# A two-block transformer kernel: x loaded in four parts between the weights and split from PSUM, the bias lines as one matmul, and the side work of the first projection in smaller steps

## The chip, the cores and the metric

One core of a Trainium2 chip runs the whole program. The metric is device time in microseconds (us) of that core, inputs in HBM to output in HBM; the kernel before has a median of 2737.01 us over 3 runs. Everything is float32 in and out. The matrix products run on TensorE (PE) as three products of split operands: a float32 number is written as hi + lo, and hi·hi, hi·lo and lo·hi are added up in PSUM. ScalarE (ACT) makes every hi, VectorE (DVE) every lo, SyncE (SP) issues the weight transfers.

## The reference, cut to what matters

The first block begins with a norm and one projection whose columns are q, k, v, u and g; the change touches this part and the small preparations for what follows it.

```python
a = rms_norm(h, attn_norm_g[i])                 # x is 256 x 2048
z = a @ w_in[i]
zq, zk, zv, zu, zg = jnp.split(z, splits, axis=-1)
...
bias = rel_bias[t5_bucket(kpos[None, :] - qpos[:, None])]   # 4 heads, depends on kpos - qpos only
logits = jnp.where(mask, logits + bias[None, :, None], NEG_INF)
...
o_gmlp = gmlp_spatial_gate(jax.nn.gelu(zu), jax.nn.gelu(zg), gmlp_ln_g[i], gmlp_ln_b[i], gmlp_ws[i], gmlp_b[i])
...
h = jnp.concatenate([meta, x], axis=1)          # second block: 16 meta tokens ahead
hn = rms_norm_2(h, norm_mix_g)
```

## The kernel before, in words

The program is a list of segments (`schedule`): `v`, `qk`, `g`, `u`, `out`, `f1_up0` and so on. A segment reads one activation buffer (`A` or `B`, hi and lo side by side) and works through its weights in pieces of 256 rows by 512 columns. One transfer from SP (`run` inside the `sync` block) brings two pieces (1 MiB) into one of 4 slots of `raw`. For each piece ACT copies `raw` to `hi` (`split` on ACT), DVE computes `lo = raw - hi` (`split` on DVE), both into rings of 4, and PE multiplies it (`piece`). In the `v` segment, the first, a piece is 12 matmuls of 512 columns, and a piece may start only when its `lo` is there. In `qk`, the second, a piece starts with its `hi`.

Every engine executes its own instructions strictly in the order written. `walk` writes that order for ACT and DVE: split up to three pieces ahead (`AHEAD`), at a group's end the evacuation, and after certain pieces the side steps that the table `SIDE` names, by segment and piece number. `run` on PE places the same side steps after the same pieces. So a side step on which PE waits holds up all matmuls behind it, and a step on which ACT waits holds up the hi of all later pieces. The `split` of piece n waits until piece n-4 has been used.

Before the first piece, x is transposed on PE to `h` (features on partitions), 32 transposes of 128x128: DVE copies PSUM to `h`, ACT makes the hi of `A` from `h` (`high_parts`), DVE the lo (`low_parts`). The gains are loaded ahead of x as nine small vectors, since `high_parts` scales by one of them.

The side steps of `v` before are these. `token_squares` and `token_rstd` make 1/rms of each token. `lines` builds for each head a line of 512 bias values, by four matmuls whose stationary operand repeats the head's 32 values 128 times; the result, the same line on all 128 partitions, goes to `line` and from there to the DRAM tensor `skew`, whose rows are 513 long. `read_bias` waits on ACT for that transfer (`skew_written`) and then reads `skew` back with a row step of 512, which shifts each row by one: this is `bias`. `row_rstd` turns 1/rms into a row, `turn_ws` transposes the gate weights and the meta tokens, `meta_rstd` makes 1/rms of the meta tokens, `lambda` the scalar of the attention.

Of the kernel before, what the change touches and what calls it, by code (L numbers as in the profile page):

```python
# [19 lines left out]
ALU = mybir.AluOpType  # L20
# [5 lines left out]
P = 128  # L26
D = 2048
# [25 lines left out]
V1N, V2N = 82, 96  # L53

# [54 lines left out]
def ffn(add, name, n, gate, up, down, kinds, layout):  # L109
# [37 lines left out]
    ("f1_up0", 6): ["ffn_rstd"], ("f1_up0", 7): ["settle"],  # L147
# [51 lines left out]
def bass_two_blocks(nc, ins, out):  # L199
    SEGS, TOTAL = schedule()  # L200

    with ExitStack() as ctx:
# [6 lines left out]
        def overlay(**shapes):  # L209
# [13 lines left out]
        line, _, = overlay(line=[P, HEADS, LINE], pad_line=[P, 1])  # L223
# [24 lines left out]
        _, relb_in, meta_in, vin1, vin2, relb, onehot, lamv, rb = overlay(  # L248
            v_skip=[P, 2048 - 8], relb_in=[32, HEADS], meta_in=[META, D], vin1=[V1N, P], vin2=[V2N, P], relb=[32, HEADS, P],
# [21 lines left out]
        consts_set, vecs_landed, early_landed = sem("consts_set"), sem("vecs_landed"), sem("early_landed")  # L271
        gmlp_normed = sem("gmlp_normed")
        left_scaled, right_scaled = sem("left_scaled"), sem("right_scaled")
        x_landed = [sem(f"x_landed{i}") for i in range(2)]
        skew_written, bias_landed, late_landed, stored = (
            sem("skew_written"), sem("bias_landed"), sem("late_landed"), sem("stored"))
        NVECS, NEARLY = 9, 9
# [28 lines left out]
        def _(sp):  # L306

            for name, src in (("attn", ins["attn_norm_g"][0]), ("ffn", ins["ffn_norm_g"][0]), ("fin", ins["final_norm_g"]),
                              ("mix2", ins["norm_mix_g_2"]), ("ffn2", ins["norm_ffn_g_2"]), ("subln", ins["subln_g"][0])):
                n = src.shape[0] // P  # L310
                sp.dma_start(vin1[V1[name]:V1[name] + n, :], src.rearrange("(k p) -> k p", p=P)).then_inc(vecs_landed, 16)
            sp.dma_start(vin2[0:32, :], ins["b_gate_2"].rearrange("(k p) -> k p", p=P)).then_inc(vecs_landed, 16)
            sp.dma_start(vin2[32:48, :], ins["pool_scale_2"].rearrange("(k p) -> k p", p=P)).then_inc(vecs_landed, 16)
            sp.dma_start(vin2[48:96, :], ins["conv_w_2"].rearrange("c (k p) -> (c k) p", p=P)).then_inc(vecs_landed, 16)
            for c in range(2):
                sp.dma_start(xtok[:, :, c * 1024:(c + 1) * 1024],
                             ins["x"][0].rearrange("(a p) d -> p a d", p=P)[:, :, c * 1024:(c + 1) * 1024]).then_inc(x_landed[c], 16)

            def small_loads():

                sp.dma_start(relb_in[:, :], ins["rel_bias"]).then_inc(early_landed, 16)
                sp.dma_start(onehot[:, :], ins["bucket_onehot"]).then_inc(early_landed, 16)
                sp.dma_start(ws_in[:, :, :], ins["gmlp_ws"][0].rearrange("g i j -> i g j")).then_inc(early_landed, 16)
                sp.dma_start(meta_in[:, :], ins["meta_tokens_2"]).then_inc(early_landed, 16)
                for j, name in enumerate(("lambda_q1", "lambda_k1", "lambda_q2", "lambda_k2")):
                    sp.dma_start(lamv[:, j, :], ins[name].to_broadcast([P, P])).then_inc(early_landed, 16)
                sp.dma_start(p_in[:, :, :], ins["p"][0, 0].rearrange("(a p) d -> p a d", p=P)).then_inc(early_landed, 16)
# [115 lines left out]
        def _(act):  # L443
# [137 lines left out]
            def side(step, G, more):  # L581
                if step == "token_squares":
                    for c in range(2):
                        act.wait_ge(x_landed[c], 16)
                    for a in range(2):
                        for b in range(2):
                            c = 2 * a + b
                            own.mark(act.activation(pb_copy[:, :, :], xtok[:, a, b * 1024:(b + 1) * 1024].rearrange("p (k t) -> p k t", k=4),
                                                    ACT.Square, accum_out=small[:, 2 + c:3 + c]))
                            wait(own)  # L590
# [3 lines left out]
                elif step == "lines":  # L594
                    pe_out.skip()
                    wait(pe_out)
                    act.activation(line[:, 0:2, :], ps[:, 2:4, :], ACT.Copy)
                    pe_in.mark(act.activation(line[:, 2:4, :], ps[:, 6:8, :], ACT.Copy))
                    wait(pe_in)

                    act.dma_start(skew[:, :, 0:LINE].rearrange("h p c -> p h c"), line[:, :, :]).then_inc(skew_written, 16)
# [6 lines left out]
                elif step == "turn_ws":  # L608
                    pe_out.skip()
                    asked.skip()  # L610
                    wait(asked)
                    given.mark(act.activation(tiny[:, 0, 0:KT * META], metaT[:, :, :].rearrange("p k t -> p (k t)"), ACT.Square))

                    act.wait_ge(pe_done, pe_out.now())
# [4 lines left out]
                elif step == "meta_rstd":  # L619
                    pe_out.skip()  # L620
                    rsqrt_start(tiny[:, 0, 0:META], tiny[:, 1, 0:META], rstd_meta[:, :])
# [23 lines left out]
                elif step == "split_meta":  # L645
                    asked.skip()
                    wait(asked)
                    given.mark(act.activation(B[:, :, 0:META], metaT[:, :, :], ACT.Copy))
                elif step == "ffn_rstd":
# [53 lines left out]

            act.wait_ge(consts_set, 2)
# [3 lines left out]
            pe_out.skip(5)  # L708
            for c in range(4):
                asked.skip()  # L710
                wait(asked)
                given.mark(high_parts(A, 4 * c, 0, lambda i: h[:, 4 * c + i:4 * c + i + 1, :], "attn"))
                ready.skip()
                if c < AHEAD:
                    split(c, c)
# [12 lines left out]
        def _(dve):  # L728
# [43 lines left out]
            def evacuate(kind, G, end, b0, gi, k, more):  # L772
                Rm = row_of(R, MT)
                if kind == "v" or kind == "g":
# [157 lines left out]
            def side(what, G, more):  # L932
                if what == "token_squares":
                    pass
                elif what == "token_rstd":
# [4 lines left out]
                elif what == "lines":  # L940
                    dve.wait_ge(early_landed, 16 * NEARLY)

                    pe_in.mark(dve.tensor_copy(relb[:, :, :], relb_in[:, :].unsqueeze(2).to_broadcast([32, HEADS, P])))
# [9 lines left out]
                elif what == "read_bias":  # L953
                    dve.wait_ge(bias_landed, 16)

                    step(dve.memset(bias[0:CHUNK, :, P + CHUNK:2 * P], NEG))
                elif what == "turn_ws":
# [4 lines left out]
                    hand(dve.tensor_copy(metaT[:, :, :], ps[:, 6, 0:KT * META].rearrange("p (k t) -> p k t", k=KT)))  # L962
                    given.skip()
                elif what == "meta_rstd":
                    wait(given)
                    pe_in.mark(dve.tensor_reduce(tiny[:, 1, 0:META], tiny[:, 0, 0:KT * META].rearrange("p (k t) -> p t k", k=KT),
                                                 AXX, ALU.add))
                    pe_out.skip()
                    wait(pe_out)
                    step(rsqrt(tiny[:, 0, 0:META], tiny[:, 1, 0:META], rstd_meta[:, :], ps[:, 7, 0:META], 1.0 / D))  # L970
                    pe_in.mark(dve.tensor_copy(r_row[:, 0:META], rstd_meta[:, :]))
# [58 lines left out]
                elif what == "split_meta":  # L1030
# [5 lines left out]
                    step(dve.tensor_tensor(B[:, :, TM:TM + META], metaT[:, :, :], B[:, :, 0:META], ALU.subtract))  # L1036
                elif what == "ffn_rstd":
# [75 lines left out]

            dve.memset(sumsq[:, :, :], 0.0)
            pe_out.skip()
            wait(pe_out)
            dve.tensor_copy(vec1[:, :], ps[:, 7, 0:V1N])
            pe_in.mark(dve.tensor_copy(vec2[:, :], ps[:, 7, P:P + V2N]))
            wait(pe_in)

            def x_low(c):
                given.skip()
                wait(given)
                ready.mark(low_parts(A, 4 * c, 0, lambda i: h[:, 4 * c + i:4 * c + i + 1, :], "attn"))


            for c in range(4):
                pe_out.skip()
                wait(pe_out)
                hand(dve.tensor_copy(h[:, 4 * c:4 * c + 4, :], ps[:, 2 * c:2 * c + 2, :].rearrange("p b (k t) -> p (b k) t", k=2)))  # L1130
                if c:
                    x_low(c - 1)
                    split(c - 1, c - 1)
            x_low(3)
# [14 lines left out]
        def _(pe):  # L1149
# [5 lines left out]

            pe.wait_ge(consts_set, 3)
            pe.wait_ge(vecs_landed, 16 * NVECS)
            pe.transpose(ps[:, 7, 0:V1N], vin1[:, :], ident[0:V1N, 0:V1N])
            done.mark(pe.transpose(ps[:, 7, P:P + V2N], vin2[:, :], ident[0:V2N, 0:V2N]))
            for k in range(KT):  # L1160
                if k % 8 == 0:
                    pe.wait_ge(x_landed[k // 8], 16)
                if k == KT - 2:
                    v_in.skip()
                    wait(v_in)
                for a in range(2):
                    last = pe.transpose(ps[:, k // 2, (k % 2) * T + a * P:(k % 2) * T + (a + 1) * P],
                                        xtok[:, a, k * P:(k + 1) * P], ident[:, :])
                if k % 4 == 3:
                    done.mark(last)  # L1170
# [224 lines left out]
```

## Time and profile before

| | |
|---|---|
| median of 3 runs | 2737.01 us (2736.24 to 2737.77) |
| profiled execution, its own time | 2737.0 us |
| its span, first to last instruction | 2735.2 us |
| PE, PEld, DVE, ACT busy | 98%, 87%, 61%, 46% |
| chain that ended last | PE 94%, DVE 4%, ACT 1%, issue 1% |
| mean granted TensorE clock | 0.994 |

PE is the time for which a matmul was in the array, PEld the loading of stationary operands beside it. The granted clock is a share of 2.4 GHz: 1.00 or 0.50 (1.2 GHz). In a timeline row stand the start, the duration, the engine, the line, the operation, and in brackets the idle time before it with what ended it. `SPq` and `ACTq` are DMA issues by those engines; the transfer itself runs on the 16 DMA engines and lands later.

### The profile page before, as it was taken

What the parts mean: (1) busy time and instruction counts of PE and PEld (TensorE: products, weight loads), DVE (VectorE), ACT (ScalarE), POOL (GpSimd) and SP (SyncE); (2) the same over time, 40 slices, a digit from 0 to 9 for tenths busy, and PEclk for the clock granted to TensorE, in tenths of its full rate; (3) what the DMA queues carried; (4) which work ended last, traced back from release to release, by engine and by line L of the source; (5) the groups of instructions that cost most, each with busy time, mean ns of one, the idle gap of its engine ahead of it and who ended that gap; (6) DMA issues with size and microseconds to landing.
All of it is one profiled execution on the core that took longest, in us unless ns stands there. A gap on an engine that the chain in (4) does not pass through costs nothing.

```text
span 2735.2 us, 40029 instructions
## 1 busy us (share of the span) xinstructions
PE 2684.0 (98%) x15696; PEld 2375.9 (87%) x15696; DVE 1673.9 (61%) x1601; ACT 1266.9 (46%) x1352; POOL 0.8 (0%) x7
## 2 busy tenths in 40 slices
PE   6998999999999999999999999999999999999998
PEld 4887988888888888888999999888888888888886
DVE  4557676555565555697576566556765655565554
ACT  4446554444444444565443333444554434443443
POOL 0000000000000000000000000000000000000000
PEclk9999999999999999999999999999999999999999
DMA  7553455555555555555545555555555555555553
GB/s 240 180 185 124 170 186 189 191 188 184 184 184 187 194 186 197 178 183 194 175 157 201 181 180 180 195 186 190 192 187 192 191 189 194 186 185 199 180 184 128
DMA packets 253102, 504.27 MB, mean 184 GB/s; under 512 B 8018, under 2 KB 10500, under 8 KB 252580
## 3 DMA queue, kind: packets, MB, share of 16 engines
q1 hardware_dynamic: 251348, 498.39, 53.5%
q10 hardware_dynamic: 1632, 4.19, 0.5%
q8 instruction: 83, 1.36, 0.2%
q14 instruction: 39, 0.32, 0.0%
HBM read 499.41 MB, written 3.15 MB: 184 GB/s over the span
## 4 chain that ended last, share of the span: by engine, by line
PE 94%; DVE 4%; ACT 1%; issue 1%; DMA 0%; SPq 0%; ACTq 0%; DVEq 0%
PE ps L1192 47%; PE ps L1198 24%; PE ps L1211 4%; PE ps L1212 4%; PE ps L1213 4%; PE ps L1230 3%; PE ps L1229 3%; PE ps L1231 3%; DVE lo L749 1%; ACT hi L465 0%; PE ps L1221 0%; PE ps L1222 0%; PE ps L1223 0%; DMA xtok<-in_x_dram 0%; PE ps L1242 0%
## 5 line engine op out<-in xcount | busy, mean ns | idle before, releaser
L749 DVE TENSOR_TENSOR lo<-raw,hi 128x1024 fp32r<-128x1024 f32 x940 | 1137.2, 1223 | 832.8 <-ACT hi L465 830.4
L465 ACT ACTIVATE hi<-raw 128x1024 fp32r<-128x1024 f32 x940 | 984.6, 1056 | 996.3 <-PE ps L1198 698.8
L1192 PE MATMUL ps<-A,hi 128*128 128x512 f32 x3648 | 914.0, 392 | 1.5 <-DVE work L757 1.5
L1192 PEld LDWEIGHTS ps<-A,hi 128*128 128x128 f32 x3648 | 656.4, 189 | 119.3 <-DVE work L757 1.7
L1198 PEld LDWEIGHTS ps<-A,lo 128*128 128x128 f32 x3648 | 497.6, 190 | 35.7 <-DVE lo L749 0.2
L1198 PE MATMUL ps<-A,lo 128*128 128x256 f32 x3648 | 508.7, 282 | 0.0
L1192 PE MATMUL ps<-B,hi 128*128 128x512 f32 x1984 | 499.6, 393 | 0.3 <-ACT hi L465 0.3
L1192 PEld LDWEIGHTS ps<-B,hi 128*128 128x128 f32 x1984 | 356.1, 188 | 66.1 <-ACT hi L465 0.5
L1198 PEld LDWEIGHTS ps<-B,lo 128*128 128x128 f32 x1984 | 269.8, 189 | 20.6
L1198 PE MATMUL ps<-B,lo 128*128 128x256 f32 x1984 | 275.6, 281 | 0.0
L1230 PE MATMUL ps<-B,hi 128*128 128x258 f32 (+1 forms) x768 | 219.5, 286 | 0.0
L1229 PE MATMUL ps<-B,hi 128*128 128x258 f32 (+1 forms) x768 | 218.5, 285 | 0.7 <-issue 0.7
L1231 PE MATMUL ps<-B,lo 128*128 128x258 f32 (+1 forms) x768 | 219.1, 285 | 0.0
L757 DVE TENSOR_TENSOR work<-ps,pb_copy 128x1024 f32<-128x1024 f32 x92 | 112.6, 1224 | 134.7 <-ACT pb_copy L484 132.9
L484 ACT ACTIVATE pb_copy<-ps 128x1024 f32<-128x1024 f32 x96 | 98.5, 1027 | 156.6 <-PE ps L1198 155.8
L1229 PEld LDWEIGHTS ps<-B,hi 128*128 128x128 f32 x768 | 145.8, 190 | 0.9 <-issue 0.9
L1231 PEld LDWEIGHTS ps<-B,lo 128*128 128x128 f32 x768 | 144.2, 188 | 0.0
L1230 PEld LDWEIGHTS ps<-B,hi 128*128 128x128 f32 x768 | 144.2, 188 | 0.0
L1211 PE MATMUL ps<-hi,B 128*128 128x512 f32 x352 | 137.0, 389 | 0.0
L1212 PE MATMUL ps<-lo,B 128*128 128x512 f32 x352 | 137.0, 389 | 0.0
L1213 PE MATMUL ps<-hi,B 128*128 128x512 f32 x352 | 136.9, 389 | 0.0
L1213 PEld LDWEIGHTS ps<-hi,B 128*128 128x128 f32 x352 | 66.1, 188 | 13.8
(211 smaller groups left out, 1317.0 us busy)
## 6 DMA issues: line engine op xcount, KB each, us to landing
raw<-in_w_in_dram SPq DMA_DIRECT2D x136, 1024.0 KB, 5.0
raw<-in_ffn_w_dram SPq DMA_DIRECT2D x132, 1024.0 KB, 5.0
raw<-in_w_gate_up_dram SPq DMA_DIRECT2D x88, 1024.0 KB, 4.8
raw<-in_w_down_dram SPq DMA_DIRECT2D x44, 1024.0 KB, 5.0
raw<-in_w_out_dram SPq DMA_DIRECT2D x16, 1024.0 KB, 5.1
raw<-in_pl_w_gate_dram SPq DMA_DIRECT2D x16, 1024.0 KB, 5.1
raw<-in_conv_out_w_dram SPq DMA_DIRECT2D x16, 1024.0 KB, 5.0
raw<-in_w_o_dram SPq DMA_DIRECT2D x16, 1024.0 KB, 5.0
```

The costliest lines, as they stand in the source:

```text
L465: act.activation(hi[:, slot % RING], raw[:, raw_slot, 2 * (slot % 2):2 * (slot % 2) + 2, :], ACT.Copy).then_inc(hi_ready, 1)
L484: act.activation(pb_copy[:, :, :], ps[:, b0:b0 + 4, T:2 * T], ACT.Copy).then_inc(copied, 1)
L749: dve.tensor_tensor(lo[:, slot % RING], raw[:, slot // 2 % RAWS, 2 * (slot % 2):2 * (slot % 2) + 2, :], hi[:, slot % RING], ALU.subtract). ...
L757: dve.tensor_tensor(to, ps[:, b0:b0 + 4, 0:T], pb_copy[:, :, :], ALU.add).then_inc(psum_free, 1)
L1192: pe.matmul(to, high(slot, kk, m), both, start=j == 0 and kk == 0, stop=False)
L1198: last = pe.matmul(ps[:, b0 + m, 0:T], low(slot, kk, m), Xh, start=False, stop=j == seg.pieces - 1 and kk == 1)
L1211: pe.matmul(to, Xh, hi[:, slot % RING, kk, :], start=first, stop=False)
L1212: pe.matmul(to, Xh, lo[:, slot % RING, kk, :], start=False, stop=False)
L1213: last = pe.matmul(to, Xl, hi[:, slot % RING, kk, :], start=False, stop=final)
L1229: pe.matmul(to, Wh, Xh, start=first, stop=False)
L1230: pe.matmul(to, Wh, Xl, start=False, stop=False)
L1231: last = pe.matmul(to, Wl, Xh, start=False, stop=final)
```

## The change

- SP: x comes as four transfers of 512 columns (0.5 MiB), one ahead of each of the first four weight transfers. The gain that the first projection needs is issued by ACT; the other eight vectors move behind the weights, into `small_loads`.
- The hi and the lo of `A` are made straight from PSUM, two 128-feature tiles at a time (`high_x`, `low_x`). Three quarters of x are turned before the first piece, the last after the third piece (`turn_x3`). The copies to `h` (`keep_x0` to `keep_x3`) become side steps.
- PE runs 12 transposes of the identity into bank 0 at the start and after each of the three quarters (`busy`).
- `lines` is one matmul with 4 output partitions; ACT copies 4 partitions, and the transfer to `skew` reads each of the 4 rows 128 times.
- `token_squares` becomes four steps; `token_rstd` moves from after piece 2 to after piece 8, with the evacuation of the first group behind it (`first_v`); `row_rstd`, `lines`, `turn_ws`, `read_bias`, `lambda` come after pieces 9, 10, 11, 12, 13. The mask of `bias` moves to `qk`, the squares of the meta tokens to `out`, and their 1/rms joins that of `f1_up0` (`first_ffn_rstd`).

```diff
 SIDE = {
-    ("v", 0): ["token_squares"], ("v", 2): ["token_rstd"], ("v", 4): ["lines"], ("v", 6): ["row_rstd"],
-    ("v", 7): ["read_bias"], ("v", 8): ["turn_ws"], ("v", 9): ["meta_rstd"],
-    ("v", 11): ["lambda"],
+    ("v", 1): ["keep_x0"], ("v", 2): ["turn_x3"], ("v", 3): ["keep_x1"], ("v", 4): ["squares0", "keep_x2"],
+    ("v", 5): ["squares1", "keep_x3"], ("v", 6): ["squares2"], ("v", 7): ["squares3"], ("v", 8): ["token_rstd", "first_v"],
+    ("v", 9): ["row_rstd"], ("v", 10): ["lines"], ("v", 11): ["turn_ws"], ("v", 12): ["read_bias"], ("v", 13): ["lambda"],
+    ("qk", 5): ["mask_bias"], ("out", 9): ["meta_squares"],
...
+                            if isinstance(n, int) and n < RAWS:
+                                load_x(n)
...
# ACT, lines
-                    act.activation(line[:, 0:2, :], ps[:, 2:4, :], ACT.Copy)
-                    pe_in.mark(act.activation(line[:, 2:4, :], ps[:, 6:8, :], ACT.Copy))
+                    pe_in.mark(act.activation(line[0:HEADS, :], ps[0:HEADS, 6, :], ACT.Copy))
                     wait(pe_in)
-
-                    act.dma_start(skew[:, :, 0:LINE].rearrange("h p c -> p h c"), line[:, :, :]).then_inc(skew_written, 16)
+                    act.dma_start(skew[:, :, 0:LINE], line[0:HEADS, :].unsqueeze(1).to_broadcast([HEADS, P, LINE])).then_inc(skew_written, 16)
...
# ACT, start
+            def high_x(u):
+
+                pe_out.skip()
+                wait(pe_out)
+                given.mark(high_parts(A, 2 * u, 0, lambda i: ps[:, X_BANK[u], i * T:(i + 1) * T].unsqueeze(1), "attn", 2))
...
# DVE
+                elif what in ("keep_x0", "keep_x1", "keep_x2", "keep_x3"):
+                    c = int(what[-1])
+                    b = X_BANK[2 * c]
+                    dve.tensor_copy(h[:, 4 * c:4 * c + 4, :], ps[:, b:b + 2, :].rearrange("p b (k t) -> p (b k) t", k=2)).then_inc(x_kept, 1)
...
+                elif what == "first_v":
+                    dve.wait_ge(pieces_used, 8)
+                    for a in range(2):
+                        last = dve.tensor_scalar(V[:, a, 0:GC], ps[:, a, :], r_tok[:, a:a + 1], None, ALU.mult)
+                    last.then_inc(psum_free, 1)
...
# PE, start
+            busy(12)
+            pe.wait_ge(gain_landed, 16)
+            done.mark(pe.transpose(ps[:, 1, 0:KT], vin1[0:KT, :], ident[0:KT, 0:KT]))
+            for c in range(3):
+                pe.wait_ge(x_landed[c], 16)
+                turn_x(2 * c)
+                turn_x(2 * c + 1)
+                busy(12)
...
# PE, sides
                 elif what == "lines":
-                    v_in.skip()
-                    wait(v_in)
-                    pe.wait_ge(to_act, 4)
-                    for hd in range(HEADS):
-                        last = pe.matmul(ps[:, (2, 3, 6, 7)[hd], :], relb[:, hd, :], onehot[:, :], start=True, stop=True)
-                    done.mark(last)
+                    pe.wait_ge(early_landed, 16 * NEARLY)
+                    pe.wait_ge(x_kept, 3)
+                    done.mark(pe.matmul(ps[0:HEADS, 6, :], relb_in[:, :], onehot[:, :], start=True, stop=True))
```

On ACT, from the write of the bias lines to their reading back, the order before is this (`hi<-raw` is the split of one piece, `raw_landed` and `pieces_used` what it waits for):

```order
L597 ACTIVATE line<-ps 128x1024 [waits pe_done]
L598 ACTIVATE line<-ps 128x1024
L601 DMA skewed_lines<-line 128x4x512 [waits s_to_pe]
L465 ACTIVATE hi<-raw 128x1024 [waits pieces_used,raw_landed0] x2
L465 ACTIVATE hi<-raw 128x1024 [waits pieces_used,raw_landed1]
L607 DMA bias<-skewed_lines 128x4x256 [waits skew_written]
L465 ACTIVATE hi<-raw 128x1024 [waits pieces_used,raw_landed1]
```

and the same stretch of the change is this:

```order
L605 ACTIVATE line<-ps 4x512 [waits pe_done]
L607 DMA skewed_lines<-line 512x1x512 [waits s_to_pe]
L470 ACTIVATE hi<-raw 128x1024 [waits pieces_used,raw_landed3]
L617 DMA bs_row<-in_gmlp_b_dram 128x1024 [waits pe_done]
L619 DMA ln_rows<-in_gmlp_ln_g_dram 128x1024
L620 DMA ln_rows<-in_gmlp_ln_b_dram 128x1024
L470 ACTIVATE hi<-raw 128x1024 [waits pieces_used,raw_landed3]
L613 DMA bias<-skewed_lines 128x4x256 [waits skew_written]
L470 ACTIVATE hi<-raw 128x1024 [waits pieces_used,raw_landed0]
```

Three splits (pieces 8, 9, 10) stood between the write and the wait for it, now two (14 and 15), and the split right behind the wait is now that of piece 16, the first of `qk`.

On PE, the start of the program before, up to the first matmul of the first piece (L1167 is a transpose of x):

```order
L1158 MATMUL ps<-ident,vin 128x82 [waits vecs_landed,consts_set]
L1159 MATMUL ps<-ident,vin 128x96
L1167 MATMUL ps<-ident,xtok 128x128 [waits x_landed0]
L1167 MATMUL ps<-ident,xtok 128x128 x15
L1167 MATMUL ps<-ident,xtok 128x128 [waits x_landed1]
L1167 MATMUL ps<-ident,xtok 128x128 x11
L1167 MATMUL ps<-ident,xtok 128x128 [waits v_to_pe]
L1167 MATMUL ps<-ident,xtok 128x128 x3
L1211 MATMUL ps<-hi,A 128x512 [waits lo_ready,act_ready,to_act]
```

and of the change, from its second quarter of x on:

```order
L1198 MATMUL ps<-ident,xtok 128x128 [waits x_landed1]
L1198 MATMUL ps<-ident,xtok 128x128 x7
L1191 MATMUL ps<-ident 128x128 x12
L1198 MATMUL ps<-ident,xtok 128x128 [waits x_landed2]
L1198 MATMUL ps<-ident,xtok 128x128 x7
L1191 MATMUL ps<-ident 128x128 x12
L1250 MATMUL ps<-hi,A 128x512 [waits lo_ready,act_ready]
```

The first piece stood behind all of x and stands now behind three quarters of it and the 12 transposes that follow the third.

## Rows read from the trace of the kernel before

**Rows 1.** The page: busy time and costliest groups (mean ns after the comma).

```profile
PE 2684.0 (98%) x15696; PEld 2375.9 (87%) x15696; DVE 1673.9 (61%) x1601; ACT 1266.9 (46%) x1352; POOL 0.8 (0%) x7
...
L749 DVE TENSOR_TENSOR lo<-raw,hi 128x1024 fp32r<-128x1024 f32 x940 | 1137.2, 1223 | 832.8 <-ACT hi L465 830.4
L465 ACT ACTIVATE hi<-raw 128x1024 fp32r<-128x1024 f32 x940 | 984.6, 1056 | 996.3 <-PE ps L1198 698.8
```

**Rows 2.** Timeline of PE, from the first transpose to the first matmul of `qk`.

```profile
10.67 5.22 PE L1167 MATMUL ps<-ident,xtok 128*128 128x128 f32 x32 [3.98 <-DMA xtok<-in_x_dram]
...
18.71 0.47 PE L1211 MATMUL ps<-hi,A 128*128 128x512 f32 x1 [2.82 <-DVE lo L749]
...
35.94 0.39 PE L1213 MATMUL ps<-hi,A 128*128 128x512 f32 x1
38.84 4.98 PE L1242 MATMUL ps<-onehot,relb 32*128 32x512 f32 x8 [2.51 <-DVE relb L943]
...
51.56 0.71 PE L1250 MATMUL ps<-ident,rb 128*128 128x128 f32 x4
52.03 0.48 PE L1211 MATMUL ps<-hi,A 128*128 128x512 f32 x1
...
57.61 1.03 PE L1256 MATMUL ps<-ident,ws_in 128*128 128x128 f32 x8
...
59.68 0.50 PE L1211 MATMUL ps<-hi,A 128*128 128x512 f32 x1
...
67.50 0.61 PE L1263 MATMUL ps<-tiny,ones 128*128 128x16 f32 x2 [4.80 <-DVE tiny L966]
67.95 0.77 PE L1211 MATMUL ps<-hi,A 128*128 128x512 f32 x1
...
80.75 0.39 PE L1211 MATMUL ps<-hi,A 128*128 128x512 f32 x1
...
86.19 1.98 PE L1192 MATMUL ps<-A,hi 128*128 128x512 f32 x8
```

**Rows 3.** Stretches of time: busy us by engine, granted clock, DMA share, GB/s.

```profile
41.00:42.00 1.00, 1.00 (x3) 0.39 (x2) 0.00 (x0) 0.00 (x0) 0.00 (x0) 0.55 1.03 395
...
64.00:66.00 2.00, 0.00 (x0) 0.00 (x0) 0.27 (x1) 1.34 (x2) 0.00 (x0) 0.75 1.08 410
```

**Rows 4.** Timeline of SP: when transfers were issued.

```profile
0.75 0.40 SPq L311 DMA_DIRECT2D vin<-in_attn_norm_g_dram  x1
...
4.69 0.94 SPq L316 DMA_DIRECT2D xtok<-in_x_dram  x2
...
22.97 28.54 SPq L355 DMA_DIRECT2D raw<-in_w_in_dram  x5
```

**Rows 5.** Timeline of ACT: first split, bias lines written, read back.

```profile
16.12 1.06 ACT L465 ACTIVATE hi<-raw 128x1024 fp32r<-128x1024 f32 x1 [0.40 <-DMA raw<-in_w_in_dram]
...
45.83 0.41 ACTq L601 DMA_DIRECT2D skewed_lines<-line  x1
...
54.97 0.37 ACTq L607 DMA_DIRECT2D bias<-skewed_lines  x1
```

**Rows 6.** Timeline of DVE: `token_rstd`, `row_rstd`, evacuation of the first group.

```profile
35.37 0.15 DVE L938 TENSOR_TENSOR small<-small 128x2 f32<-128x2 f32 x1
...
36.69 0.16 DVE L930 SCALAR_TENSOR_TENSOR small<-small 128x2 f32<-128x2 f32 x1
...
51.03 0.48 DVE L947 TENSOR_SCALAR rb<-ones,small 128x128 f32<-128x128 f32 x2
...
55.09 1.41 DVE L777 TENSOR_SCALAR V<-ps,small 128x512 f32<-128x512 f32 x2 [1.09 <-PE ps L1213]
```

**Rows 7.** DMA packets of all queues, first 7.0 us.

```profile
DMA packets 355, 0.28 MB, mean 41 GB/s; under 512 B 130, under 2 KB 308, under 8 KB 355
```

**Rows 8.** ACT's queue (packets, MB, share of 16 engines) in 46.5:48.5, then 48.5:51.5.

```profile
q10 hardware_dynamic: 313, 0.64, 95.7%
...
q10 hardware_dynamic: 142, 0.28, 97.6%
```

More of the change, by code:

```diff
@@ L53 @@
 V1N, V2N = 82, 96
+X_BANK = (2, 3, 4, 5, 6, 7, 2, 3)
 class Segment:
@@ L306, in _, with load_x @@
         def _(sp):
[L308 to L317, printed above, removed]
+            def load_x(c):
+                sp.dma_start(xtok[:, :, c * GC:(c + 1) * GC],
+                             ins["x"][0].rearrange("(a p) d -> p a d", p=P)[:, :, c * GC:(c + 1) * GC]).then_inc(x_landed[c], 16)
             def small_loads():
@@ L581, in side @@
             def side(step, G, more):
[L582 to L590, printed above, removed]
+                if step == "turn_x3":
+                    high_x(6)
+                    high_x(7)
+                    ready.skip()
+                elif step in ("keep_x0", "keep_x1", "keep_x2", "keep_x3", "first_v", "mask_bias", "meta_squares"):
+                    pass
+                elif step in ("squares0", "squares1", "squares2", "squares3"):
+                    c = int(step[-1])
+                    a, b = c // 2, c % 2
+                    own.mark(act.activation(pb_copy[:, :, :], xtok[:, a, b * 1024:(b + 1) * 1024].rearrange("p (k t) -> p k t", k=4),
+                                            ACT.Square, accum_out=small[:, 2 + c:3 + c]))
+                    wait(own)
                 elif step == "token_rstd":
@@ L701, in side @@
                             ready.skip()
+            def high_x(u):
+                pe_out.skip()
+                wait(pe_out)
+                given.mark(high_parts(A, 2 * u, 0, lambda i: ps[:, X_BANK[u], i * T:(i + 1) * T].unsqueeze(1), "attn", 2))
+            act.dma_start(vin1[0:KT, :], ins["attn_norm_g"][0].rearrange("(k p) -> k p", p=P)).then_inc(gain_landed, 16)
             act.wait_ge(consts_set, 2)
             own.mark(act.activation(small[:, 57:58], ones[:, 0:1], ACT.Copy))
[L708 to L712, printed above, removed]
+            pe_out.skip()
+            asked.skip()
+            wait(asked)
+            for c in range(3):
+                high_x(2 * c)
+                high_x(2 * c + 1)
                 ready.skip()
-                if c < AHEAD:
-                    split(c, c)
+                if c == 0:
+                    split(0, 0)
+                if c < 2:
+                    split(c + 1, c + 1)
             def last():
@@ L773, in evacuate @@
                 Rm = row_of(R, MT)
+                if kind == "v" and gi == 0:
+                    return
                 if kind == "v" or kind == "g":
@@ L953, in side @@
                 elif what == "read_bias":
+                    pass
+                elif what == "mask_bias":
                     dve.wait_ge(bias_landed, 16)
@@ L961, in side @@
                     step(dve.memset(wsT[CHUNK:P, :, 0:CHUNK], 0.0))
[L962 to L971, printed above, removed]
+                    dve.tensor_copy(vec1[:, :], ps[:, 7, 0:V1N])
+                    dve.tensor_copy(vec2[:, :], ps[:, 7, P:P + V2N])
+                    pe_in.mark(dve.tensor_copy(metaT[:, :, :], ps[:, 6, 0:KT * META].rearrange("p (k t) -> p k t", k=KT)))
+                    wait(pe_in)
+                elif what == "meta_squares":
+                    step(dve.tensor_tensor(tiny[:, 0, 0:KT * META], metaT[:, :, :].rearrange("p k t -> p (k t)"),
+                                           metaT[:, :, :].rearrange("p k t -> p (k t)"), ALU.mult))
+                    step(dve.tensor_reduce(rstd_meta[:, :], tiny[:, 0, 0:KT * META].rearrange("p (k t) -> p t k", k=KT),
+                                           AXX, ALU.add))
                 elif what == "lambda":
@@ L1036, in side @@
                     step(dve.tensor_tensor(B[:, :, TM:TM + META], metaT[:, :, :], B[:, :, 0:META], ALU.subtract))
+                elif what == "first_ffn_rstd":
+                    b = 4 * ((G + 1) % 2)
+                    pe_out.skip()
+                    wait(pe_out)
+                    step(rsqrt(tiny[:, 0, :], tiny[:, 1, :], r_row[:, :], ps[:, b, 0:TM], 1.0 / D,
+                               lambda: pe_in.mark(dve.memset(sumsq[:, :, :], 0.0))))
+                    wait(pe_in)
                 elif what == "ffn_rstd":
@@ L1111, in side, with low_x @@
                             step(last)
+            def low_x(u):
+                given.skip()
+                wait(given)
+                return low_parts(A, 2 * u, 0, lambda i: ps[:, X_BANK[u], i * T:(i + 1) * T].unsqueeze(1), "attn", 2)
             dve.memset(sumsq[:, :, :], 0.0)
@@ L1116, in _ @@
             wait(pe_out)
[L1117 to L1134, printed above, removed]
+            hand(dve.tensor_copy(vec1[:, 0:KT], ps[:, 1, 0:KT]))
+            dve.wait_ge(to_act, asked.now())
+            pe_out.skip(6)
+            for c in range(3):
+                low_x(2 * c)
+                ready.mark(low_x(2 * c + 1))
+                if c == 0:
+                    split(0, 0)
+                if c < 2:
+                    split(c + 1, c + 1)
             def last():
@@ L1246, in side @@
                     wait(v_in)
-                    s_in.skip()
-                    wait(s_in)
+                    pe.wait_ge(x_kept, 4)
                     for a in range(2):
@@ L1254, in side @@
                     wait(v_in)
+                    s_in.skip()
+                    wait(s_in)
+                    pe.transpose(ps[:, 7, 0:V1N], vin1[:, :], ident[0:V1N, 0:V1N])
+                    pe.transpose(ps[:, 7, P:P + V2N], vin2[:, :], ident[0:V2N, 0:V2N])
                     for g in range(8):
@@ L1259, in side @@
                     done.mark(last)
-                elif what == "meta_rstd":
                     v_in.skip()
-                    wait(v_in)
-                    done.mark(pe.matmul(ps[:, 7, 0:META], ones[:, :], tiny[:, 1, 0:META], start=True, stop=True))
+                elif what == "first_ffn_rstd":
+                    b = 4 * ((G + 1) % 2)
+                    pe.wait_ge(act_ready, seg.reads[2] + 4)
+                    pe.wait_ge(psum_free, G)
+                    pe.matmul(ps[:, b, 0:META], ones[:, :], rstd_meta[:, :], start=True, stop=True)
+                    done.mark(pe.matmul(ps[:, b, META:TM], ones[:, :], sumsq[:, 0, :], start=True, stop=True))
                     v_in.skip()
```

75 lines of the change are left out of this document (41 added, 34 removed).

## The prediction

> **What bounds the kernel now.** The page comes first: PE is busy for 98% of the span [rows 1], so only time in which PE stands still, or computes what a neighbour could, can be won. The timeline of PE then shows where it stands still, and in the part that the change touches that is much. `v` has 16 pieces; a piece is 12 matmuls, and from 80.75 to 86.19 two of them take 5.44 us, 2.72 each [rows 2]. The segment needs 16 x 2.72 = 43.5 us and lasts from 18.71 to 86.19, 67.5 us [rows 2]. The 24.0 us over it are read off the same rows. The first five pieces take 17.5 us (18.71 to 36.17, the last matmul's start and 0.23) for 13.6: 3.9 go in waits for their lo. `lines` costs 36.17 to 43.8, 7.6 us, of which 2.5 are a wait for DVE and 5.0 the matmuls. `row_rstd` costs 0.5 (51.56 to 52.03), `turn_ws` 2.1 (57.61 to 59.68), `meta_rstd` 5.4 (4.80 idle and 0.61) [rows 2]. Nearly all the rest is the clock: the granted clock fell to 0.5 (1.2 GHz) during the `lines` matmuls, after 2.5 us of idling and then work on 32 rows only, and again in the idle 4.8 us ahead of `meta_rstd` [rows 2, 3]. The matmuls behind each ran slow at first: two pieces took 7.7 us (43.8 to 51.56) for 5.4, and the last six 18.2 (67.95 to 86.19) for 16.3, so 1.9 to 2.3 each time. After `v` nothing of size changes, so I ask one question: when does PE start `qk`, 86.19 before [rows 2]?
>
> **The start.** The first x transfer, 1 MiB, was issued at 4.69 and the first transpose ran at 10.67; two MiB more had landed at 16.12, when the first split ran [rows 2, 4, 5]. That is 2.72 us per MiB and 3.3 us fixed. The change issues x at about 0.75, where the vectors' first issue stood [rows 4], and PE needs three quarters of x, which lie behind two weight transfers: 3.5 MiB, landed at 0.75 + 3.3 + 9.5 = 13.5. Eight transposes at 0.163 (5.22/32) take 1.3, the 12 of `busy` 2.0 [rows 2]. The first piece starts at 16.8 instead of 18.7. By then pieces 0 to 2 are split, so the 3.9 us of waits go as well. The price of `busy` is 2.0 here; its copies ahead lie in waits for x.
>
> **The side steps on PE.** Turning the last quarter costs 8 transposes and a wait, 1.4. `token_rstd` now begins when DVE has made the lo of piece 12, and that needs piece 8 used: call this moment T. Hi takes 1.06, lo 1.22 with an overlap, T + 2.3 [rows 1]; the 1/rms chain from 35.37 to 36.85 adds 1.5 [rows 6]; `first_v` adds 1.41 and the row operand of `row_rstd` 0.48 [rows 6], with hand-overs T + 5.9. Piece 9 ends at T + 2.72. So PE stands for 3.2 us before `row_rstd` and works 0.5 on it: the stall moves, it does not go. `lines` is one matmul of four; eight records took 4.98 us, more than half at half clock, so one at full clock is about 0.9, with its start 1.0 [rows 2]. `turn_ws` costs 2.1 and two more transposes, 2.5. `meta_rstd` is gone and leaves one small matmul in `f1_up0`, 0.3. The copies to `h` (four of about 1.2, the size of a lo [rows 1]) and the squares fall to DVE and ACT, one per piece: 2.4 us per piece on each against 2.72 on PE, hidden; without that cover each would cost its own 1.2. The 17 small loads delay the fifth weight transfer, issued at 22.97 before [rows 4] and about then again, since the queue starts 4 us earlier and has eight issues more of some 0.47 each (x's two took 0.94 [rows 4]). Piece 8 is split when piece 4 is used, 16.8 + 13.6 + 1.4 = 31.8, so this is hidden.
>
> The sum without the transfer of the lines: 16.8 + 43.5 + 1.4 + 3.7 + 1.0 + 2.5 = 68.9. `qk` would start 17.3 us earlier.
>
> **The transfer to skew.** This term decides. Before, it was issued at 45.83 and ACT read it back at 54.97: 9.1 us to landing [rows 5]. In the change it is issued after pieces 0 to 10, the turn, `row_rstd` and `lines`: 16.8 + 29.9 + 1.4 + 3.7 + 1.0 = 52.8, plus 0.8 for the copy, 53.6. Two splits later ACT waits for it, and behind it in ACT's order stand the issue for `bias` (0.4) and the hi of piece 16 (1.06), on which PE waits. So `qk` starts at 53.6 + D + 1.5, D being the time to landing; it is hidden up to D = 13.8.
>
> What is D? The source is now 4 partitions instead of 128. Rows 7 show how transfers of few rows are spread: the nine vectors have 178 rows of 512 bytes, and 130 packets were shorter than that, the completions. Eight vectors with 16 completions and the two-row one with 2 make 130: a transfer with two rows used two engines. With four source rows I expect 4 engines, 128 packets of 2 KB each. Of packet times the rows give two: 313 in 95.7% of 32 engine-us, 98 ns; and 142 in 97.6% of 48, 330 ns, when the writes stalled [rows 8]. With the fixed 3.3 that is D = 15.8 or 45.5. A second bound: a sixteenth of the memory's partitions never moved more than a sixteenth of 410 GB/s [rows 3], 25.6 GB/s. Whether the engine or the side of the partitions sets this the trace of before can't tell, since both were always spread alike. If it is the engine, 1.05 MB take 10.2 us over four; if it is the partitions, four neighbours have one sixteenth's rate, 41.0 us, and D is 43.9 with the issue and landing of some 2.9. I take the second: the mildest reading must assume that partitions which never gave more than an eighth of 25.6 GB/s each can give eight times that, and the stalled packets point to the same size.
>
> The Trainium skill speaks against this edit twice. "DMA: Bandwidth & Descriptors" (Why a DMA increments its semaphore by 16 and not by 1) says that the number of engines is the largest up to 16 that divides the slowest dimension of both sides: 4 here, and the two completions of the two-row vector agree [rows 7]. "SBUF — State Buffer" (Door 1: The DMA port swizzle) has partitions 0 to 3 on one port and gives 27.6 GB/s for 1 MiB through it; no row here shows that. By its figure D would be an estimated 38 us and the time 2746.
>
> With D = 43.9 `qk` starts at 99.0, 12.8 later than before. PE idles 30 us; the clock fell in the idle 4.8 us before, and coming back cost 1.9 [rows 2, 3]. Sum: +12.8 + 1.9 + 0.3 = +15.0. The profiled execution took 2737.0 us beside its span of 2735.2, the median of the runs is 2737.01, so nothing has to be shifted: **2752 us**. ACT's wait also holds `lambda`, but piece 16 at half clock covers it; `bias` itself is touched only five pieces into `qk`, 13.6 us after PE goes on.
>
> **Rivals.**
> - *The engines are the limit* (faster). Four engines at 98 ns a packet, D = 15.8: `qk` at 70.9, -15.3 + 0.3, 2722. For it: 84 to 98 ns is all that packets need when nothing stalls them. Against it: nothing shows one partition feeding an engine alone. With the mean of all stretches, about 160 ns, D = 24, -7.3 + 1.9, 2732, within reach of no change. It decides below D = 23.4.
> - *The transfer isn't confined* (faster). All 16 engines, D about 9, hidden: 2720. Against it are rows 7.
> - *The stall at `row_rstd` also drops the clock*. The clock fell in an idle 4.8 us, and after an idle 2.5 only once matmuls on 32 rows ran [rows 2, 3]; 3.2 lie between: +1.9 in each case above, 2754 with mine.
> - *x lands later than its share*, because small packets of the gain and four more issues sit between: 1 to 2 us on the start, whole in the faster cases, and also in mine, as the lines are then written later.
>
> **How the numbers follow.** A measurement of this kernel can't tell less than about 0.2%, 5.5 us. Slower by that means D above 34, faster means D below 23.4. My forecast (D from 36 to 48) has a chance of 0.58, its own range is 2744 to 2757. Four free engines have 0.24, the unconfined transfer 0.06, D between 23 and 34 has 0.10, anything else 0.02. So slower 0.60, same 0.10, faster 0.30. The range must reach both signs: 2721, under the four engines, to 2757, the forecast with a second clock drop and D of 47.
>
> **What would show it.** In the trace of the changed kernel: the first matmul of a piece at 16.8 (13.5 for the third quarter's transposes); idle 3.2 us before `row_rstd`; `lines` 0.9 us; the issue of the skew transfer at 53.6 and of `bias` D later; ACT idle before that issue, PE idle ahead of its first `qk` matmul with the hi of piece 16 as releaser, at 99; the clock at 0.5 around it. The forecast is wrong if `bias` is issued before 77, and the sum of the rest is wrong if the last `v` matmul doesn't end near 69.

## The result, and the profile after

The changed kernel takes 2754.42 us (2753.44 to 2756.32, 4 runs) beside 2737.39 (2736.24 to 2738.01): a ratio of 1.0059, 95% interval 1.0047 to 1.0071. It is slower by 17 us, and the interval excludes 1; 2752 was forecast. The profiled execution took 2753.85 us, its span is 2752.1.

The page of the changed kernel, its busy times and the two lines of its chain (the work that ended last) that answer to the question:

```profile
PE 2689.7 (98%) x15739; PEld 2383.6 (87%) x15739; DVE 1672.8 (61%) x1597; ACT 1263.0 (46%) x1347; POOL 0.8 (0%) x7
...
PE 94%; DVE 2%; DMA 2%; ACT 1%; issue 0%; SPq 0%; ACTq 0%; DVEq 0%
PE ps L1231 46%; PE ps L1237 24%; PE ps L1250 4%; PE ps L1252 4%; PE ps L1251 4%; PE ps L1269 3%; PE ps L1268 3%; PE ps L1270 3%; DMA skewed_lines<-line 2%; DVE lo L762 1%; PE ps L1260 0%; PE ps L1261 0%; PE ps L1262 0%; DMA xtok<-in_x_dram 0%; ACT hi L470 0%
```

Busy time alone says nothing here, PE is at 98% in both. The chain does: a DMA now has 2% of the span, and it is the write of the bias lines. The chain in order of time gives its start and length:

```profile
53.51 43.21 DMA skewed_lines<-line
```

The timeline of ACT shows what stood behind it (L607 writes the lines, L613 reads them back, L470 is a split):

```profile
52.89 0.59 ACT L605 ACTIVATE line<-ps 4x512 f32<-4x512 f32 x1 [7.51 <-PE ps L1285]
53.51 1.25 ACTq L607 DMA_DIRECT2D skewed_lines<-line  x1
54.86 1.06 ACT L470 ACTIVATE hi<-raw 128x1024 fp32r<-128x1024 f32 x1 [1.38 <-issue]
58.00 10.23 ACTq L617 DMA_DIRECT2D bs_row<-in_gmlp_b_dram  x1
68.26 3.75 ACTq L619 DMA_DIRECT2D ln_rows<-in_gmlp_ln_g_dram  x1
72.38 3.44 ACTq L620 DMA_DIRECT2D ln_rows<-in_gmlp_ln_b_dram  x1
75.93 1.06 ACT L470 ACTIVATE hi<-raw 128x1024 fp32r<-128x1024 f32 x1 [20.00 <-issue]
96.75 0.39 ACTq L613 DMA_DIRECT2D bias<-skewed_lines  x1
97.24 1.06 ACT L470 ACTIVATE hi<-raw 128x1024 fp32r<-128x1024 f32 x1 [20.26 <-DMA skewed_lines<-line]
```

The split at 97.24 is that of piece 16, and the wait ahead of it ends with the transfer. And the timeline of PE, where it stood still or where a piece began:

```profile
14.39 1.47 PE L1191 MATMUL ps<-ident 128*128 128x128 f32 x12
15.62 0.47 PE L1250 MATMUL ps<-hi,A 128*128 128x512 f32 x1
...
46.98 1.22 PE L1291 MATMUL ps<-ident,rb 128*128 128x128 f32 x4 [2.98 <-DVE rb L972]
47.85 0.77 PE L1250 MATMUL ps<-hi,A 128*128 128x512 f32 x1
...
51.84 1.02 PE L1285 MATMUL ps<-onehot,relb_in 32*4 32x512 f32 x2
...
78.35 0.79 PE L1250 MATMUL ps<-hi,A 128*128 128x512 f32 x1 [12.00 <-DVE lo L762]
...
98.44 3.42 PE L1231 MATMUL ps<-A,hi 128*128 128x512 f32 x8 [14.60 <-ACT hi L470]
...
102.66 2.00 PE L1231 MATMUL ps<-A,hi 128*128 128x512 f32 x8
```

The first piece starts at 15.62 (18.71 before), piece 11 starts at 52.79, when it was forecast (by misses that cancel, see below), and then PE stands 12.00 and 14.60 us. `qk` starts at 98.44 instead of 86.19 [rows 2]: 12.3 us of the 16.9 by which the spans differ. Its first piece takes 4.2 us instead of 2.8, which is 1.4 more: the granted clock was 0.50 from 98 to 100 and 0.66 from 100 to 102. The last 3 us lie far behind the change. About half of them, 1.5, come from a single place, the piece behind an idle 1.78 us at 1148.64. The granted clock was 0.81 from 1148 to 1150 and 0.50 from 1150 to 1152, and in the same place before it was 1.00 (the 8 matmuls took 2.13 us behind an idle 1.79):

```profile
1148.64 3.29 PE L1231 MATMUL ps<-PT,hi 128*128 128x512 f32 x8 [1.78 <-DVE UP L770]
```

Whether this belongs to the change isn't settled. In the traces of the experiments below these 8 matmuls took 2.12 us in `e1`, 2.13 in `e8` (the old order), and 2.5 to 3.7 in the six others. From the start of `qk` to the end of the span it is 2649.0 us in both traces of the old order and 2649.2 to 2654.0 in the eight of the new one, while the times of one kernel differ by up to 3.3 us (2736.49 to 2739.79).

### The profile page after: what moved, and what is told of

It is laid out like the page before. It is cut to its first block, busy times and chain, and to the rows that moved or that the text cites. A ratio compares the mean times of both kernels' runs of the same rounds, so it can differ in the third digit from the quotient of the medians.

```text
span 2752.1 us, 40112 instructions
## 1 busy us (share of the span) xinstructions
PE 2689.7 (98%) x15739; PEld 2383.6 (87%) x15739; DVE 1672.8 (61%) x1597; ACT 1263.0 (46%) x1347; POOL 0.8 (0%) x7
## 4 chain that ended last, share of the span: by engine, by line
PE 94%; DVE 2%; DMA 2%; ACT 1%; issue 0%; SPq 0%; ACTq 0%; DVEq 0%
PE ps L1231 46%; PE ps L1237 24%; PE ps L1250 4%; PE ps L1252 4%; PE ps L1251 4%; PE ps L1269 3%; PE ps L1268 3%; PE ps L1270 3%; DMA skewed_lines<-line 2%; DVE lo L762 1%; PE ps L1260 0%; PE ps L1261 0%; PE ps L1262 0%; DMA xtok<-in_x_dram 0%; ACT hi L470 0%
## 5 line engine op out<-in xcount | busy, mean ns | idle before, releaser
L470 ACT ACTIVATE hi<-raw 128x1024 fp32r<-128x1024 f32 x940 | 984.7, 1057 | 1028.0 <-PE ps L1237 695.9
L1231 PE MATMUL ps<-A,hi 128*128 128x512 f32 x3648 | 915.5, 393 | 16.1 <-ACT hi L470 14.6
```

What stands on the lines that cost most here:

```text
L470: act.activation(hi[:, slot % RING], raw[:, raw_slot, 2 * (slot % 2):2 * (slot % 2) + 2, :], ACT.Copy).then_inc(hi_ready, 1)
L1231: pe.matmul(to, high(slot, kk, m), both, start=j == 0 and kk == 0, stop=False)
```

## The experiments

All give one thing to read, the start of `qk` on PE, besides the time. The theory is that the side of the four neighbouring partitions limits the transfer; the rival is that the four engines do.

**e1: each line on all 128 partitions again, still by one matmul.** DVE repeats each head's values 32 times (the copy waits for the small loads, after piece 7), and ACT copies all 128 partitions of the result.

```diff
+ pe_in.mark(dve.tensor_copy(relw[:, :].rearrange("b (h r) -> b h r", h=HEADS), relb_in[:, :].unsqueeze(2).to_broadcast([32, HEADS, P // HEADS])))
...
- done.mark(pe.matmul(ps[0:HEADS, 6, :], relb_in[:, :], onehot[:, :], start=True, stop=True))
+ done.mark(pe.matmul(ps[:, 6, :], relw[:, :], onehot[:, :], start=True, stop=True))
...
- act.dma_start(skew[:, :, 0:LINE], line[0:HEADS, :].unsqueeze(1).to_broadcast([HEADS, P, LINE])).then_inc(skew_written, 16)
+ act.dma_start(skew[:, :, 0:LINE].rearrange("h (r c) l -> (h r) c l", c=HEADS),
+               line[:, :].unsqueeze(1).to_broadcast([P, HEADS, LINE])).then_inc(skew_written, 16)
```

> One matmul still makes the bias lines, but each head's 32 values stand 32 times in the stationary operand, so all 128 partitions hold a line and the skew transfer reads each of 128 partitions 4 times instead of each of 4 partitions 128 times. Both theories on why it is slow (the four neighbouring partitions, or the four engines) expect the same here: landing in 9 to 14 us instead of 43.2, the bias issue no longer ends a wait of ACT that PE feels, qk from about 69 instead of 98.4, and a time of 2723 us (2720 to 2726). If something else than this transfer made the changed kernel slow, it stays above 2740.

Measured: 2722.16 us (2720.35 to 2722.97) beside 2738.13, ratio 0.9938, interval 0.9922 to 0.9955. ACT's DMA issues in its timeline, then the first matmul of `qk`:

```profile
54.97 0.59 ACTq L607 DMA_DIRECT2D skewed_lines<-line  x1
59.43 0.37 ACTq L618 DMA_DIRECT2D bs_row<-in_gmlp_b_dram  x1
59.83 0.46 ACTq L620 DMA_DIRECT2D ln_rows<-in_gmlp_ln_g_dram  x1
60.66 0.33 ACTq L621 DMA_DIRECT2D ln_rows<-in_gmlp_ln_b_dram  x1
62.36 0.39 ACTq L614 DMA_DIRECT2D bias<-skewed_lines  x1
```

```profile
70.35 1.98 PE L1235 MATMUL ps<-A,hi 128*128 128x512 f32 x8
```

The read-back follows 7.4 us behind the write, sooner than the 9 to 14 expected, and ACT did not wait for it. The three issues take 0.3 to 0.5 us again, and behind `row_rstd` PE waits nowhere up to `qk`. So the whole loss hung on this one transfer, and the rest of the change is worth 16 us.

**e2: the same four partitions, 16 engines.** One transfer per head; the read-back waits for all four.

```diff
- act.dma_start(skew[:, :, 0:LINE], line[0:HEADS, :].unsqueeze(1).to_broadcast([HEADS, P, LINE])).then_inc(skew_written, 16)
+ for hd in range(HEADS):
+     act.dma_start(skew[hd:hd + 1, :, 0:LINE], line[hd:hd + 1, :].unsqueeze(1).to_broadcast([1, P, LINE])).then_inc(skew_written, 16)
```

> The source stays on partitions 0 to 3, but the transfer is issued as four, one per head, whose slowest dimension is 128 on both sides, so that each should spread over 16 engines. If the side of the partitions is the limit (my theory), nothing changes: about 43 us from the first issue to the reading back, time near 2754. If the four engines were the limit (rival), it lands in about 10 us and the time is near 2723. Completion packets tell whether 16 engines took part: 16 for each transfer instead of 4.

Measured: 2749.47 us (one run). ACT's timeline:

```profile
53.63 17.71 ACTq L608 DMA_DIRECT2D skewed_lines<-line  x4
71.80 9.15 ACTq L618 DMA_DIRECT2D bs_row<-in_gmlp_b_dram  x1
80.99 9.60 ACTq L620 DMA_DIRECT2D ln_rows<-in_gmlp_ln_g_dram  x1
90.62 0.48 ACTq L621 DMA_DIRECT2D ln_rows<-in_gmlp_ln_b_dram  x1
93.83 0.39 ACTq L614 DMA_DIRECT2D bias<-skewed_lines  x1
```

From the first issue to the read-back it is 40.2 us, as the partition theory has it. That more engines took part shows in the DMA answers (packets, MB, share of 16 engines' time) for stretches in which no other queue was busy: `e2` from 56 to 60, and below the changed kernel from 62 to 66.

```profile
DMA packets 52, 0.11 MB, mean 27 GB/s; under 512 B 0, under 2 KB 0, under 8 KB 52
...
q10 hardware_dynamic: 52, 0.11, 87.7%
```

```profile
DMA packets 50, 0.10 MB, mean 26 GB/s; under 512 B 0, under 2 KB 0, under 8 KB 50
...
q10 hardware_dynamic: 50, 0.10, 23.1%
```

In the changed kernel ACT's queue held 23.1% of 16 engines, 3.7 of them, busy with 26 GB/s. In `e2` it held 87.7%, 14 engines, and the bytes came no faster, 27 GB/s: the busy share of the engines counts time in which they get nothing done. PE stood 10.40 and 14.90 us, ahead of pieces 14 and 15, and started `qk` at 98.53, as late as in the changed kernel (98.44). That the time was 5 us below the 2754 expected arose behind this start, in one run, and isn't explained beyond the first piece of `qk`, which ran at full clock here (1.4 us).

**e3: four engines, four partitions far apart.** The lines of the heads stand on partitions 0, 36, 72 and 108 (the other columns of the stationary operand are zero; ACT copies all 128 partitions, the transfer reads these four).

```diff
+ step(dve.memset(relw[:, :], 0.0))
+ pe_in.mark(dve.tensor_copy(relw[:, 0:109:36], relb_in[:, :]))
...
- act.dma_start(skew[:, :, 0:LINE], line[0:HEADS, :].unsqueeze(1).to_broadcast([HEADS, P, LINE])).then_inc(skew_written, 16)
+ act.dma_start(skew[:, :, 0:LINE], line[0:109:36, :].unsqueeze(1).to_broadcast([HEADS, P, LINE])).then_inc(skew_written, 16)
```

> The mirror image: one transfer with four source rows, so four engines, but the heads' lines stand on partitions 0, 36, 72 and 108. The partition theory expects packets of 84 to 98 ns in place of 290, landing in 14 to 18 us, qk from about 70 and a time of 2722 to 2727. The engine theory expects no change: 43 us, 2754.

Measured: 2723.25 us (one run). ACT's timeline, and ACT's queue from 55 to 58:

```profile
53.67 1.24 ACTq L607 DMA_DIRECT2D skewed_lines<-line  x1
...
68.51 0.39 ACTq L613 DMA_DIRECT2D bias<-skewed_lines  x1
```

```profile
q10 hardware_dynamic: 144, 0.29, 25.8%
```

The transfer takes 14.8 us, 4.1 engines are busy, and 144 packets in 25.8% of 48 engine-us (16 engines for 3 us) are 86 ns each, where the neighbouring partitions gave 50 in 23.1% of 64, 296 ns. With `e2` this settles it, though each is a single run (the effect, 31 us of time, is ten times what single runs differ): spreading the partitions takes 28.4 us off the transfer (43.2 to 14.8), raising the number of engines 3.0 (43.2 to 40.2).

**e4: the slow transfer kept, the wait moved behind.**

```diff
- ("v", 12): ["read_bias"], ... ("qk", 5): ["mask_bias"]
+ ("qk", 13): ["read_bias"], ("qk", 15): ["mask_bias"]
```

> The skew transfer stays as slow as in the changed kernel, but ACT waits for it and reads it back only after piece 13 of qk, and the mask follows after piece 15. The wait for the transfer then costs nothing, but the three issues behind it on ACT's queue (10.2, 3.8 and 3.4 us in the changed kernel) still hold up the hi of piece 15. Expected: PE idle some 12 us before piece 15, qk from about 83 instead of 98.4, time 2738 to 2741. If the issues are slow only because of something else, or if the wait weren't the cause, the time would be near 2723 or stay at 2754.

Measured: 2737.98 us (one run), the time of the kernel before. ACT's issues and PE's two starts, piece 15 and `qk`:

```profile
56.60 10.20 ACTq L617 DMA_DIRECT2D bs_row<-in_gmlp_b_dram  x1
66.83 3.74 ACTq L619 DMA_DIRECT2D ln_rows<-in_gmlp_ln_g_dram  x1
70.95 3.41 ACTq L620 DMA_DIRECT2D ln_rows<-in_gmlp_ln_b_dram  x1
```

```profile
76.89 0.79 PE L1250 MATMUL ps<-hi,A 128*128 128x512 f32 x1 [11.93 <-DVE lo L762]
...
82.17 2.27 PE L1231 MATMUL ps<-A,hi 128*128 128x512 f32 x8
```

A transfer whose landing PE never waits for still makes PE stand 12 us, because ACT stands in the issues behind it. In time, `e4` is 15.8 us above `e1`, and the changed kernel another 16.4 above `e4` (1.4 of these because the clock fell ahead of piece 10 in the changed kernel and not in `e4`). So the slow transfer had two prices in the changed kernel, 12.0 us of idle PE by the issues and 14.6 by the wait.

There is a third, which the changed kernel doesn't pay, as no split waits for weights behind this stretch. A weight transfer from SP that is issued while the slow one runs also lands late. These are two answers for the stretch from 77 to 79 (KB, us from issue to landing), of the changed kernel, then of `e1`:

```profile
raw<-in_w_in_dram SPq DMA_DIRECT2D x1, 1024.0 KB, 22.9
```

```profile
raw<-in_w_in_dram SPq DMA_DIRECT2D x1, 1024.0 KB, 4.9
```

In `e4` four such transfers took 17.9 to 22.9 us, ACT waited 10.45 us for the weights (until 99.80) and PE for ACT:

```profile
101.00 2.08 PE L1231 MATMUL ps<-A,hi 128*128 128x512 f32 x8 [1.64 <-ACT hi L470]
```

That they queue behind the slow packets on the engines that both use fits these rows; no run tests it by itself.

**e5: `e1` with `lines` and `row_rstd` exchanged.**

```diff
- ("v", 9): ["row_rstd"], ("v", 10): ["lines"]
+ ("v", 9): ["lines"], ("v", 10): ["row_rstd"]
```

> The wide lines of e1 (2722.2), and lines and row_rstd change places: lines after piece 9, row_rstd after piece 10. In e1 PE stood 2.98 us ahead of row_rstd for its operand and ran at half clock behind it. The operand is ready some 3 us after piece 9 ends; with lines (1.0) and piece 10 (2.7) in between, the wait goes. Expected: no idle time ahead of row_rstd, clock at 1.0 there, qk from about 66 instead of 70.3, 2718 us (2716 to 2720). The rival, that another wait (of ACT for the lines, or of DVE for the row) takes its place: 2721 to 2723.

Measured: 2717.58 us (2717.01 to 2719.65) beside 2737.98, ratio 0.9924, interval 0.9907 to 0.9940. The row operand's wait, in PE's timeline:

```profile
49.13 0.71 PE L1298 MATMUL ps<-ident,rb 128*128 128x128 f32 x4 [1.19 <-DVE rb L976]
```

It shrank from 2.98 to 1.19 us and didn't vanish, but the matmuls around it run at full clock, and `qk` starts at 65.68, 4.7 us earlier than in `e1`. Of these 1.8 are the idle time and most of the rest is the clock. This is the fastest version found. The six traces with the idle 2.98 us differ in what followed: from the start of piece 10 to `lines` it is 5.4 us in `e1`, 3.9 to 4.2 in the changed kernel, `e2`, `e3` and `e6`, and 2.9 in `e4`, where the granted clock stayed at 1.00.

**e6: `e1` without `busy`.** The body of `busy` is left out; it computes nothing that is used.

> e1 without any of the 48 transposes of busy. If they do nothing but take time, the first piece starts 1.2 us earlier (14.4 instead of 15.6) at full clock and the time is 2721. If they are what raises the clock before the first piece (transposes of the changed kernel stood 0.22 us apart until 9.2 us and 0.12 after), the transposes of x stay slow and the first matmuls run at half clock for a few us, costing 2 to 4: 2723 to 2726.

Measured: 2724.61 us (one run). PE's timeline for the third quarter of x and the first piece, of `e6`, then of `e1`:

```profile
13.46 1.97 PE L1201 MATMUL ps<-ident,xtok 128*128 128x128 f32 x8 [2.10 <-DMA xtok<-in_x_dram]
15.08 0.78 PE L1253 MATMUL ps<-hi,A 128*128 128x512 f32 x1
```

```profile
13.41 1.09 PE L1202 MATMUL ps<-ident,xtok 128*128 128x128 f32 x8 [1.66 <-DMA xtok<-in_x_dram]
14.33 1.47 PE L1195 MATMUL ps<-ident 128*128 128x128 f32 x12
15.56 0.47 PE L1254 MATMUL ps<-hi,A 128*128 128x512 f32 x1
```

Without `busy` the 8 transposes take 1.97 us instead of 1.09 and the first matmuls are slow, so the first piece starts 0.5 us earlier, and by the fourth matmul it is 0.15 us behind `e1` (16.48 and 16.33). In this execution `qk` started at 69.19, in `e1` at 70.35, because the clock was low for longer ahead of `e1`'s `lines`. The one time is 2.5 us above `e1`'s median and within what single runs differ. Whether `busy` pays is not settled by this. That it raises the clock early is shown: the third quarter's 8 transposes took 1.09 or 1.10 us in every trace with `busy`, and 1.97 in the one without.

**e7: `e5` without the last 12 transposes.**

```diff
+ if c < 2:
      busy(12)
```

> e5 without the last 12 transposes of busy, the only ones on the path. Expected: the clock is up by then and stays, the first piece starts at 14.4 instead of 15.6 and the kernel gains 1.2 us on e5: about 2717. If the clock falls for want of them, it loses 1 to 3 us on e5.

Measured: 2718.54 us (2717.02 to 2719.08), ratio 0.9926, interval 0.9909 to 0.9943. `qk` started at 64.39, 1.3 us earlier than in `e5`, as expected; the times of the two can't be told apart.

**e8: the kernel before with the lines alone.** One matmul, 4 partitions copied, the transfer from partitions 0 to 3; all else as before.

> The kernel before with one part of the change alone: one matmul for the lines, 4 partitions copied, and the transfer to skew from partitions 0 to 3. By the partition theory the transfer lands after 40 to 43 us instead of 9.1, ACT stands that much longer in read_bias, the squares of the meta tokens behind it come later, and PE waits for them ahead of piece 10: about +29 us less a few, 2758 to 2768. If the transfer is slow only in company of the new order, the time is 2733 to 2738 (4 us of lines saved, some of it clock).

Measured: 2764.88 us (one run). ACT's timeline, and PE's, ahead of piece 10:

```profile
40.28 1.24 ACTq L600 DMA_DIRECT2D skewed_lines<-line  x1
...
83.58 0.41 ACTq L606 DMA_DIRECT2D bias<-skewed_lines  x1
```

```profile
95.67 0.61 PE L1260 MATMUL ps<-tiny,ones 128*128 128x16 f32 x2 [39.01 <-DVE tiny L965]
```

The transfer takes 43.3 us in the old order as well, which pays 27 us for it. The chain is the expected one with a link more: DVE masks `bias` ahead of copying the meta tokens, so it too waits for the read-back (37.09 us), and only then come the squares, on which PE waits.

```profile
87.54 0.27 DVE L955 MEMSET bias<- 64x256 f32 x1 [37.09 <-DMA bias<-skewed_lines]
```

The new order pays what its other parts had won and 17 more.

## Why the prediction was right

- *The start* was forecast at 16.8 and came at 15.6. The mean of 0.163 us that I took for a transpose mixed two paces: with the clock up it is 0.12 (8 in 0.93, 14.39 less 13.46), so the turn and the last `busy` took 2.2 us and not 3.3. The last quarter's turn took 0.8 for a forecast 1.4.
- *The stall ahead of `row_rstd`* was forecast at 3.2 and measured 2.98. The clock did fall in it, the case given as a rival: the piece behind took 3.9 us (47.85 to 51.8) instead of 2.7, and the matmuls of `row_rstd` 0.9 instead of 0.5. These losses and the two gains above nearly cancel, and the skew transfer was issued at 53.51; forecast 53.6. That this agrees to 0.1 us is luck.
- *`lines`* took 1.0 us as forecast.
- *D*, the term that decides, was forecast at 43.9 and measured 43.2, and its mechanism, the side of the partitions against the number of engines, is shown by `e2` and `e3`. The bound for it from the sixteenth of 410 GB/s [rows 3], 25.6 GB/s, is close to the rate that the trace has, 26. The second support, the stalled packets of 330 ns, is close to the 296 ns measured but was no evidence for them: those packets came on ACT's queue at 97.6% of all 16 engines, from 128 partitions, at 0.28 MB in 3.0 us [rows 8], and what stalled them no run here shows. The packet time of 98 ns [rows 8] was right for four free engines: 86 ns in `e3`, D of 14.8 where 15.8 was worked out.
- *The start of `qk`* was forecast at 99.0 and came at 98.44; the clock's return was forecast at 1.9 and cost 1.4.
- *What the prediction missed* is the queue. It gave ACT's three issues no time; they took 17.4 us, which alone delayed piece 15 by 12. That changed nothing here only because the wait for the transfer ended later still. By the prediction's own sign, a last `v` matmul that doesn't end near 69, its sum of the rest was wrong: it ended at 83.8, since piece 15 came late (in `e1`, with fast issues, `v` ends at 70.35). The rival with D near 24 leaves the issues out as well. How long they would have taken there, between the 2.2 us of `e3` (D of 14.8) and 17.4, no run shows, so its 2732 may be too low.
- *The remaining 3 us* late in the program were not in the sum. It had 0.3 for `f1_up0`, where the added matmul took 0.14 (422.53 to 422.67). Whether the rest comes with the change is open, as said above. Up to the end of `qk`'s first piece the change cost 13.7 us, where 14.7 was forecast (12.8 and 1.9).

The two rules of the Trainium skill named in the prediction hold in this case. "DMA: Bandwidth & Descriptors" (Why a DMA increments its semaphore by 16 and not by 1) has the slowest dimension decide the number of engines: a source of four rows kept 3.7 of 16 busy. The Trainium skill's page "SBUF — State Buffer" (Door 1: The DMA port swizzle) gives 27.6 GB/s for partitions 0 to 3; the trace has 26. By the same section of the Trainium skill's page, partitions 0, 36, 72 and 108 lie on four different ports, and `e3` took 14.8 us instead of 43.2.

## What to carry to other kernels

A DMA that reads a few rows many times can be much slower than one that reads many rows a few times (43.2 us against 7.4 here, for the same bytes written). Ask how many partitions the source has, and whether they are neighbours, before you replace work that puts data on 128 partitions by a read that repeats. A slow transfer costs at the wait for it, at every later issue into its queue, and at other transfers that land late beside it; look at the duration of the issues on that engine and at the landing times, not only at who waits for this landing. And when one bundle of edits is slower, read the chain for a new entry first: here the rest of the bundle was worth -16 us (`e1` against the kernel before) and one transfer +32 (2754.4 against 2722.2).

## What the runs showed of the hardware

- Four neighbouring partitions gave 26 GB/s to 4 DMA engines and 27 to 14 (packets of 2 KB took 296 ns on four); four partitions 36 apart gave 86 ns per packet and 98 GB/s (144 packets, 0.29 MB in 3 us).
- The three issues on ACT took 0.3 to 0.5 us each in `e1`, and 3.4 to 10.2 us behind the slow transfer in the changed kernel. A weight transfer issued by SP in the same time landed after 22.9 us instead of 4.9.
- The same idle 2.98 us on PE was followed by a granted clock of 0.50 in five of six traces and of 1.00 in the sixth (`e4`), and an idle 1.19 us by 1.00 in both traces that have it (`e5`, `e7`). One trace says little on whether a stall of this size drops the clock.
- The column of the granted clock says 1.00 for the first us of every trace, and the first transposes nevertheless ran at the slow pace: here is the start of the changed kernel, 12 transposes in 2.8 us, and the third dozen in 1.5.

```profile
1.67 2.82 PE L1191 MATMUL ps<-ident 128*128 128x128 f32 x12 [1.67 <-POOL ident L388]
...
10.32 1.47 PE L1191 MATMUL ps<-ident 128*128 128x128 f32 x12
```

At the start of a trace, read the clock from the pace of equal instructions.
